# A two-layer decoder trunk on one core: own raw places for the second hidden sub-block, norm sums moved behind three embedding panels, the last gate taken by token groups

## The reference

```python
for i in range(DEPTH):
    ...                                            # mixer and residual
    h = h + mlp_sq_relu(rmsnorm(h, norm_mlp[i]), w_up[i], w_down[i])
    gate = jax.nn.sigmoid(rmsnorm(h, norm_ple[i]) @ w_ple_gate[i])
    h = h + gate * (p[i] @ w_ple_proj[i])
return rmsnorm(h, norm_final)
```

## Time and profile before

| | us |
|---|---|
| median of three runs | 2699.61 (2699.54 to 2705.09) |
| the profiled execution | 2699.06 |
| its span, first to last instruction | 2697.5 |
| PE busy | 2530.8 (94%) |
| PEld busy | 2073.8 (77%) |
| DVE busy | 1887.4 (70%) |
| ACT busy | 1130.1 (42%) |
| POOL busy | 807.0 (30%) |

### The profile page before, as it was taken

How to read it: one execution, slowest core, us unless ns; L and a number is a source line. 1 busy time by engine, 2 the same in 40 slices (tenths; PEclk the granted TensorE clock), 3 DMA queues, 4 the chain that set the end, 5 groups by cost and what they waited for, 6 DMA issues and landing times.

```text
span 2697.5 us, 32348 instructions
## 1 busy us (share of the span) xinstructions
PE 2530.8 (94%) x11796; PEld 2073.8 (77%) x11796; DVE 1887.4 (70%) x2544; ACT 1130.1 (42%) x1830; POOL 807.0 (30%) x599
## 2 busy tenths in 40 slices
PE   7999999899999899996999999989999989999786
PEld 6788888787888678885878888878788867878675
DVE  7677555757666798996665657765766679989645
ACT  6555433434444434444342323453444444434432
POOL 2000000033232556666210000003423246666523
PEclk9999999999999999998999999999999999999998
DMA  3001010123334233321221111022333332323111
GB/s 135 25 24 32 24 32 16 55 70 110 114 106 136 99 115 105 113 82 55 83 89 40 32 32 31 24 71 70 106 107 112 131 107 94 122 97 102 55 55 70
DMA packets 79597, 207.59 MB, mean 77 GB/s; under 512 B 8608, under 2 KB 12720, under 8 KB 79456
## 3 DMA queue, kind: packets, MB, share of 16 engines
q1 hardware_dynamic: 76512, 195.85, 21.7%
q0 software_dynamic: 2224, 7.54, 0.8%
q10 hardware_dynamic: 720, 2.36, 0.2%
HBM read 163.25 MB, written 42.47 MB: 76 GB/s over the span
## 4 chain that ended last, share of the span: by engine, by line
PE 56%; issue 18%; DVE 16%; ACT 4%; POOL 3%; DMA 2%; DVEq 0%; ACTq 0%; POOLq 0%; SPq 0%
PE gemm_ps L668 8%; PE gemm_ps L670 8%; PE gemm_ps L669 8%; PE s_ps L668 7%; PE s_ps L670 7%; PE s_ps L669 7%; DVE wlo L2128 3%; PE to_ps L670 3%; PE to_ps L669 3%; PE to_ps L668 3%; DMA hid_raw<-hidden 2%; DVE b_blocks_lo L2222 2%; POOL hid_raw L1150 2%; DVE a_blocks L2222 2%; PE to_ps L774 1%
## 5 line engine op out<-in xcount | busy, mean ns | idle before, releaser
L668 PE MATMUL gemm_ps<-a_hi,whi 128*128 128x512 f32 x1024 | 424.8, 415 | 20.6 <-DVE a_lo L1745 10.8
L670 PE MATMUL gemm_ps<-a_hi,wlo 128*128 128x512 f32 x1024 | 403.3, 394 | 0.0
L669 PE MATMUL gemm_ps<-a_lo,whi 128*128 128x512 f32 x1024 | 401.9, 393 | 0.0
L668 PEld LDWEIGHTS gemm_ps<-a_hi,whi 128*128 128x128 f32 x1024 | 194.6, 190 | 61.2 <-issue 20.5
L1150 POOL TENSOR_TENSOR hid_raw<-hid_raw 128x512 f32<-128x512 f32 x128 | 208.8, 1641 | 108.3 <-DVE a_blocks L2222 44.7
L2128 DVE TENSOR_TENSOR wlo<-wraw,whi 128x512 fp32r<-128x512 f32 (+1 forms) x204 | 206.7, 1013 | 33.2 <-ACT whi L1498 32.8
L670 PEld LDWEIGHTS gemm_ps<-a_hi,wlo 128*128 128x128 f32 x1024 | 193.4, 189 | 43.1
L669 PEld LDWEIGHTS gemm_ps<-a_lo,whi 128*128 128x128 f32 x1024 | 194.6, 190 | 32.7 <-issue 1.4
L2128 DVE TENSOR_TENSOR wlo<-wraw_a,whi 128x512 fp32r<-128x512 f32 (+1 forms) x204 | 178.4, 874 | 36.5 <-ACT whi L1498 35.4
L1072 POOL COPY sumsq<-zs 128x512 f32<-128x512 f32 x12 | 16.3, 1369 | 619.1 <-ACT zs L1461 559.7
L668 PE MATMUL s_ps<-a_blocks,whi 128*128 128x512 f32 x448 | 177.9, 397 | 23.0 <-DVE wlo L2128 10.4
(11 more groups left out here) (365 smaller groups left out, 6308.6 us busy)
## 6 DMA issues: line engine op xcount, KB each, us to landing
wraw<-panels SPq DMA_DIRECT2D x90, 512.0 KB, 3.6
hid_raw<-hidden SPq DMA_DIRECT2D x128, 256.0 KB, 4.0
wraw<-folds SPq DMA_DIRECT2D x60, 512.0 KB, 4.3
wraw_a<-folds SPq DMA_DIRECT2D x60, 512.0 KB, 4.3
hidden<-sumsq SPq DMA_DIRECT2D x64, 256.0 KB, 3.5
hidden<-zs SPq DMA_DIRECT2D x32, 256.0 KB, 2.1
hidden<-zt SPq DMA_DIRECT2D x32, 256.0 KB, 2.0
h<-x_t SPq DMA_DIRECT2D x11, 512.0 KB, 5.0
```

Of the source, the lines that this page charges most:

```text
L668: nc.tensor.matmul(out, hi_w, hi_x, start=start, stop=False, skip_group_check=True)
L669: nc.tensor.matmul(out, hi_w, lo_x, start=False, stop=False, skip_group_check=True)
L670: return nc.tensor.matmul(out, lo_w, hi_x, start=False, stop=stop, skip_group_check=True)
```

## The change

- **Raw places.** Sub-block 1 gets raw places of its own: B11 and B12 in `wraw[:, 1]`, B21 and B22 in `wraw_a2`. The raw weights of turns with two pieces are packed into the other half of the weight places. Sub-block 2 follows sub-block 0 in `hid_raw`. `RAMP` splits sub-block 1 in turns 15 and 16, beside sub-block 0, and sub-block 2 from slot (16, 5).
- **Copies.** The first A and E products of turns 16 to 19 are copied by ACT instead of DVE (`first_copy`).
- **Turn 0 of each layer.** The last splits of the up-projection's input come one slot earlier, and on DVE ahead of `out_of`.
- **Tail.** Tiles 0 and 1 are split in slots 4 and 6 of turn 31, tiles 2 and 3 in slots 1 and 3 of turn 33, tiles 4 and 5 before the last `out_of`. The additions for q = 1 go to slot 3 of turn 32. ACT squares tiles 0 and 1 before it makes the high parts of tiles 6 and 7.
- **Norm sums.** They stand behind three of the four embedding panels (six of eight units). ACT makes weight parts between the squares; DVE scales the first gate panel ahead of the last embedding panel's copies.
- **Last gate and final norm (layer 1).** The last four gate tiles are done by token groups of 512, 256 and 256: for each group all four tiles, twelve units in all. Their weight parts are kept in `a_hi`. The sums and the root of a group follow while the next is computed; POOL no longer scales; DVE scales group 0's tiles between later units. The last square goes straight into the sum by a second matmul, without POOL. There are twelve output DMAs.

```diff
-RAMP = {... (15, 4): [(0, 3)], (15, 5): [(0, 4), (0, 5)], (15, 6): [(0, 6), (1, 0)], ...
+RAMP = {(15, 2): [(0, 0)], (15, 3): [(0, 1), (0, 2)], (15, 4): [(0, 3), (1, 0)], (15, 5): [(0, 4), (0, 5), (1, 1)],
+        (15, 6): [(0, 6), (1, 2)], (16, 0): [(1, 3)], (16, 1): [(1, 4)], (16, 2): [(1, 5)], (16, 3): [(1, 6)],
+        (16, 5): [(2, 0)], (16, 6): [(2, 1)], (17, 0): [(2, 2)], (17, 1): [(2, 3)],
+        (17, 2): [(2, 4)], (17, 3): [(2, 5)], (17, 4): [(2, 6)]}
+EARLY_TILES = {(LAST - 2, 4): 0, (LAST - 2, 6): 1, (LAST, 1): 2, (LAST, 3): 3}
+GROUPS_LATE = [(0, HALF), (HALF, HALF // 2), (HALF + HALF // 2, HALF // 2)]
+SCALED = {6: (0,), 7: (1, 2), 8: (3,), 9: (4,), 10: (5, 6), 11: (7,)}
+ROOTED = {5: 0, 9: 1, 11: 2}
...
@@ SP @@
+                    elif s == 1:
+                        sp.wait_ge(blk_lo_ready, BLOCKS * (turn_of(layer, UPS - 2 if name in ("B11", "B12") else UPS - 1) + 1))
...
                     load_raw(n + 2)
+                    if n >= UPS - 2:
+                        for name in ("B11", "B12") if n == UPS - 2 else ("B22", "B21"):
+                            load_hidden(1, name)
                     store(n, B_RAW["B11"], C11, 1, c11_stored)
                     if n == UPS - 1:
-                        for name in ("B11", "B12", "B22", "B21"):
-                            load_hidden(1, name)
+                        load_hidden(2, "B11")
                     store(n, B_RAW["B22"], C22, 2, c22_stored)
+                load_hidden(2, "B12")
+                load_hidden(2, "B22")
                 store(UPS - 1, B_RAW["B12"], C12[(UPS - 1) % 2], 3, c12_stored[(UPS - 1) % 2])
+                load_hidden(2, "B21")
...
@@ PE, rest_of_layer @@
-                pe.wait_ge(fold_read, reads(layer, TURNS))
-                norm_sums(st["norm"] + 2, to_ps)
                 for j in range(4):
+                    if j == 3:
+                        pe.wait_ge(fold_read, reads(layer, TURNS))
+                        norm_sums(st["norm"] + 2, to_ps)
...
@@ PE, after layer 1 @@
+            for k in range(LATE_UNITS):
+                _, c, size = late_tile(k)
+                pe.wait_ge(w_lo_ready, FIRST_LATE + k % LATE + 1)
+                pe.wait_ge(unit_free, 2 * FIRST_LATE + k - 1)
+                for kk in range(KT):
+                    w = slice(kk * P, (kk + 1) * P)
+                    last = product(gemm_ps[:, k % 2, 0:size], late_hi(k % LATE)[:, w], late_lo(k % LATE)[:, w],
+                                   b_hi[:, kk, c:c + size], b_lo[:, kk, c:c + size], kk == 0, kk == KT - 1)
+                last.then_inc(unit_ready, 1)
+                if k % LATE == 1 and k > LATE:
+                    late_sums(k // LATE - 1)
+            late_sums(len(GROUPS_LATE) - 1)
...
@@ POOL @@
+                        if n == LAST - 1 and j == 3:
+                            tail_adds(1)
                         x_sums(n, j)
...
                     if n == LAST - 1:
+                        tail_adds(2)
                         for o in range(2):
                             tile_squares(st["norm"] + 2, Idx(o), o == 0)
...
@@ ACT @@
+                def first_copy(n, j):
...
+                        A(SUM_U2[q], BANKS[n % 2]["A"], ACT.Copy).then_inc(p_copied, 1)
...
+                for o in (4, 5):
+                    for half in range(2):
+                        next_hi(o, half)
+                for o in (0, 1):
+                    for half in range(2):
+                        tail_square(o, half)
+                for o in (6, 7):
+                    for half in range(2):
+                        next_hi(o, half)
...
-                for o in range(KT):
+                for o in range(2, KT):
                     for half in range(2):
                         tail_square(o, half)
+                    if o in (3, 5):
+                        w_hi(Idx(st["gate"] + 2 + (o - 3) // 2))
+                w_hi(Idx(st["gate"] + 4))
+                w_hi(Idx(st["gate"] + 5))
                 norm_root_of(st["norm"] + 2, to_ps)
...
@@ DVE @@
-                out_of(LAST, BLOCKS - 1)
                 for o in range(4, KT):
+                    if o == 6:
+                        out_of(LAST, BLOCKS - 1)
                     for half in range(2):
                         split_of(o, half)
...
                 for j in range(4):
+                    if j == 3:
+                        norm_scale(n - 1)
+                        for half in range(2):
+                            gate_in(Idx(st["gate"]), half)
...
+            for k in range(LATE_UNITS):
+                take(k)
+                if k < LATE_UNITS - 2:
+                    add_gated(k)
+            for k in (LATE_UNITS - 2, LATE_UNITS - 1):
+                add_gated(k)
+            for n in range(1, len(GROUPS_LATE)):
+                final(n, range(KT))
```

332 lines of the change are left out of this document (222 added, 110 removed), and 3 rows, old and new, of the table RAMP.

## The result

The changed kernel takes 2658.56 us, the median of four runs (2656.14 to 2662.65), against 2700.6 for four runs of the kernel before. The ratio is 0.984, 95% interval 0.982 to 0.986: 42 us gained where 65 were forecast. 2634 was the forecast, 2608 to 2656 its range, so the result lies 2.6 us above the range. The profiled execution took 2656.41, its span is 2654.7, its clock 0.989.

The account below looks back on a forecast made before the run. PE is busy 94% of the span, so only stretches where it stands or runs slowly can give much. Gains 19.2 + 0 + 1.3 + 35.7 + 9.0 = 65.2 us from 2699.06 give 2633.9, hence 2634 for the median; range 2608 to 2656.

Parts of the forecast that it names:

- Part 1, turns 16 and 17: MLP ramp: own raw places and ACT's copies bring both turns from 36.8 to 29.2 us, near DVE's own work; 7.6 gained.
- Part 1, turn 18: Turn 18 loses its 1.4 us wait on the copy and part of its load wait; 2.0 us gained a layer.
- Part 2: Turn 0: same splits in another order before DVE's evacuation of block 4; 0 gained, bounds -3 to +3.
- Part 3, turn 32: Turn 32 loses six tile splits, POOL's additions slow weight splits; 10.5 us, 4.1 and 2.8 gained.
- Part 3, the rest: Turn 33 goes to 15.1 us, 2.4 lost in all; first gate panel from 11.9 to 13.5, 3.2 lost in two layers.
- Part 4: Norm sums behind six units: gate's end to second panel takes 24.1 us instead of 41.7 and 42.2; 35.7 gained.
- A wait for wlo: Sign that the prediction is wrong: a wait for wlo or sumsq inside the embedding.
- rival (d): Norm sums still wait, as ACT's weight parts between squares wait for embedding panels; 5 us a layer, 2644; chance 0.1.
- Part 5: The end: 12.5 us behind PE's last panel matmul instead of 24.6, 3.1 lost in PE's stream; net 9.0 gained.
- The rule of the Trainium skill: Last gate's 256-column matmuls: loads overlap only for another row group, 216 ns each, sum 18 us higher, 2652; rival's chance 0.03.
- (a): MLP waits only change hands: turns 16 to 18 gain 3 a layer, part 3 loses 5; 2654; chance 0.12.
- The bounds: Gain limits: part 1 8 to 32 us, part 3 -8 to +14; all terms at their low bounds give 31 gained.

Follow-up runs that it names:

- copies_on_dve: Changed kernel with the first A and E products of turns 16 to 19 copied by DVE again instead of ACT; 2661.83 us, ratio 0.9858.
- loads_ahead: Changed kernel with SP's loads of B11 and B12 of sub-block 3 issued ahead of turn 19's raw weights; 2651.28 us, ratio 0.9814.
- turn0_before: Changed kernel with ACT's and DVE's order in turn 0 of each layer put back to the kernel before; 2662.57 us, ratio 0.9863.
- p_load_later: Changed kernel with POOL's load of p_raw issued behind the additions for q = 1 in turn 32, not at turn 31's end; 2641.46 us.
- one_wait: Changed kernel with POOL's four additions for q = 1 beginning only after DVE's split of block 3 of turn 32; 2646.93 us.
- shifted_sums: p_load_later with POOL's two weight sums held by a wait, given four times, on PE's last product of turn 31; 2644.43 us.
- tiles_before: adds_back with the tile splits also at their places of the kernel before, in turns 32 and 33; 2649.91 us.
- sums_first: Changed kernel with each layer's norm sums back ahead of the four embedding panels, early squares of tiles 0 and 1 kept; 2683.95 us, ratio 0.9932.
- adds_paced: Changed kernel with each of the four additions for q = 1 waiting for DVE's next weight split of turn 32; 2649.87 us, ratio 0.9807.
- adds_back: Changed kernel with POOL's additions for q = 1 back at the end of turn 31, tile splits keeping new places; 2646.44 us, ratio 0.9795.

## Why the prediction was wrong, point by point

- **Part 1, turns 16 and 17: right mechanism, term too large** (7.6 a layer, measured 5.0 and 5.1). DVE is busy in nearly all of these turns, 29.7 of 31.8 us, against 28.2 of 29.2 in my working. Moving the relu steps or the squares did not shorten turn 16; PE then waited elsewhere. That DVE's operations with two sources in SBUF take 1.18 to 1.77 us beside POOL instead of 0.68 is in the traces; whether fewer of them would help is not tried. ACT's copies, which I had priced at 2.7, carry 3.2 and 4.4 (copies_on_dve).
- **Part 1, turn 18: the step failed** ("part of the wait on its load" was to vanish; +2.0 and +3.0 came instead of -2.0). I took the load as freed because sub-block 2 was split sooner. It hangs on its place in SP's queue, behind weights that wait for turn 17. loads_ahead shows it: issued ahead of them, turn 18 is 3.2 and 4.0 us shorter.
- **Part 2: a small miss.** Forecast 0; the two turns came out 3.7 us shorter together than in the kernel before, and turn0_before puts the order at 1.3 to 3.2 a layer, where the same code alone spreads over 2.4. I looked only at block 4's move. The 2.8 us before turn 0 lie in unchanged code; over the profiles of all changed versions, with the same code ahead of it, turn 0 of layer 0 starts between 596.0 and 601.1, so they are within the spread.
- **Part 3, turn 32: the step that failed most.** "It keeps POOL's 6 us of additions for q = 1, now in slot 3, which slow the weight splits there, so not 9.5 but 10.5." It took 17.55 and 17.35: the additions did not slow the splits one by one, they kept one split out for 6.25 us. Without the DMA issue directly ahead, or with DVE let in before the additions, it is as I wrote: 10.0 to 10.5 (p_load_later, one_wait, shifted_sums). I had counted POOL's operations and not what POOL's queue holds ahead of them. In the kernel before, POOL idled 0.91 us between that DMA issue and the additions, waiting for DVE.
- **Part 3, the rest: turn 33 right, the gate panel put too long.** Turn 33 was put at 15.1 and took 14.8 and 15.0. The first gate panel was put at 13.5 and took 11.8 and 11.6, 3.7 us better in two layers: squares and splits ran side by side. tiles_before shows that the new places of the splits are worth 5.2 and 5.6 us over turns 32, 33 and this panel.
- **Part 4: right mechanism, 1.6 us a layer too short.** 24.1 forecast, 25.7 measured, at a clock of 1.00 instead of 0.80. "A wait for wlo" did not come; two waits of 1.38 and 0.27 us on DVE's copies out of `s_ps` did, which the sum had at nothing. sums_first shows 24 to 25 us for the place of the sums; rival (d) is out.
- **Part 5: right, by its terms.** 12.5 forecast behind the last panel matmul, 12.1 measured; 3.1 forecast for PE's stream, 3.5 measured (79.9 against 76.4 from the second panel's first matmul to the end of the last panel matmul). Matmuls of 256 columns start 0.12 apart:

```profile
2642.07 0.28 PE L732 MATMUL gemm_ps<-b_hi,a_hi 128*128 128x256 f32 x1
2642.19 0.28 PE L733 MATMUL gemm_ps<-b_lo,a_hi 128*128 128x256 f32 x1
2642.31 0.28 PE L734 MATMUL gemm_ps<-b_hi,a_hi 128*128 128x256 f32 x1
...
2645.22 6.89 DVE L2619 SCALAR_TENSOR_TENSOR h<-h,gcol,rstd 128x256 f32<-128x256 f32 x16
```

  The last line is the new end: sixteen scalings, 0.43 each where I had put 0.34, the first eight of which hide the last root. The rule of the Trainium skill (TensorE: Matmul & The Clock Gate, "What overlaps and what doesn't"), by which the kernel would have come to 2652, does not hold here: the weight loads take 0.19 each and the matmuls still start 0.12 apart. That 2652 lies nearer to 2658.6 than my 2634 is chance, the miss is elsewhere.
- **The rivals.** (a), 2654, is nearest in time, and turns 16 to 33 did lose, 4.3 us in both layers together. But waits that change hands all over the ramp are not what happened: turns 16 and 17 gained 10.1, and two single places, turns 18 and 32, lost 11.9.
- **The bounds.** Part 1 came out at 5.1 us gained, below its low bound of 8, and part 3 at 8.5 lost, below its bound of -8, which allowed for slowed splits of 1.69 us and not for one kept out by a whole row. All terms at their low bounds add up to 28 us gained, not to the 31 of the prediction.

## What to carry to other kernels

Before work is moved on an engine's queue, read what stands directly ahead of it there, DMA issues too: a DMA issue on POOL followed at once by its vector work kept DVE out for as long as that row lasted, up to 6.25 us. When a turn becomes shorter, look for the transfers whose issue hangs on its end: they come closer to the turn that reads them by as much. And a part whose end is a chain of single operations can be forecast to a microsecond from their rows; what meets on a shared port can't, so price the meeting from both ends.

## What the runs showed of the hardware

**A row of POOL directly behind its DMA issue kept DVE out.** Elsewhere DVE gets in between two operations of POOL. In the trace of the changed kernel 160 operations of DVE with two inputs in SBUF began while an addition or subtraction of POOL ran that had the next one directly behind it (under 0.06 us), and had to wait. All but two got in as soon as that one operation had ended; the two are the 6.25 us splits. In the kernel before it is all of 163, in shifted_sums all of 173. Where the row stood 0.02 us behind a DMA issue, and DVE's split began within the issue or the row's first operation, it waited for the whole row, in both layers each time: 6.25 us through six operations, 5.79 through the issue and four, and 1.38 through two (one_wait, adds_paced). In adds_back POOL waited 0.55 us between its DMA issue and the row, and DVE got in each time. What in POOL holds the port is not shown, nor whether it is the issue itself or that the row's instructions stand ready behind it without a wait, nor whether the kind of DMA matters.

The Trainium skill (SBUF — State Buffer, "Who interferes with whom") says of DVE's modes with two ports that whichever of the two engines issues first holds the shared ports for its whole instruction, while the other is blocked, and that an operation of DVE with two inputs in SBUF contends with one of GpSimd that reads SBUF. The waits that ended after one operation agree; the rows behind a DMA issue go beyond it.

It also infers that a two-source operation of DVE does not meet the writing of DMA descriptors by GpSimd. The traces are divided. Splits that had begun ahead of an issue did their work beside it, as in shifted_sums, where the addition ahead ended at 2495.07:

```profile
2493.60 1.47 POOL L1270 TENSOR_TENSOR h<-h,sumsq 128x512 f32<-128x512 f32 x1
2495.02 0.75 POOL L1293 DMA_DIRECT2D p_raw<-p_t  x1
...
2494.44 0.92 DVE L2305 TENSOR_TENSOR wlo<-wraw_a,whi 128x256 fp32r<-128x256 f32 x1
```

But the 5.79 us split above began 0.24 us into an issue that ran on for 0.51 us, and such a split takes 0.41 alone: it should have been done just before the row began, and was not. So the numbers agree with the inference for a split that came before the issue and speak against it for this one.
